# A mixture-of-experts stage: gate and upper layer in three rounded terms with the tokens stationary

## The reference

```python
def hier_moe(x, w_rg, b_rg, w_re, b_re, w1, w3, w2):   # w1, w3: 32 x 1024 x 512, w2: 32 x 512 x 1024
    ...                                                # each token goes to 2 of 32 experts
    def block(args):
        tids, e, w = args
        xb = x_pad[tids]
        hdn = jax.nn.silu(xb @ w1[e]) * (xb @ w3[e])
        return (hdn @ w2[e]) * w[:, None].astype(xb.dtype)
```

## Time and profile before

| | us |
|---|---|
| median of 3 runs | 5024.19 |
| lowest and highest | 5019.49, 5027.0 |
| the profiled execution, its time | 5025.35 |
| its span, first to last instruction | 5024.0 |

### The profile page before, as it was taken

One profiled execution on the slowest core, in us unless ns is written; L12 is line 12 of the kernel. 1 busy time (PEld: TensorE's weight loads), 2 busy tenths in 40 slices (PEclk: granted clock), 3 DMA queues, 4 the chain that ended last, 5 costly groups with the idle time before them and its releaser, 6 DMA issues. The chain is left out here.

```text
span 5024.0 us, 53141 instructions
## 1 busy us (share of the span) xinstructions
PE 4263.0 (85%) x22050; PEld 3515.6 (70%) x22051; DVE 2141.6 (43%) x3609; ACT 1321.3 (26%) x2379; POOL 199.9 (4%) x149
## 2 busy tenths in 40 slices
PE   7877998998887998999777788888499986888884
PEld 5676677777675677777546688888476666888883
DVE  4653334333654234333444455454422243554544
ACT  3202223233202223232432222222222221222222
POOL 0000000000000000000000111111000001111110
PEclk9755579999755569999788899999795577999997
DMA  3100002222100002222003587777320015777783
GB/s 114 51 34 1 1 17 84 84 84 68 52 34 0 1 3 81 84 86 87 24 17 111 204 283 274 276 271 267 109 92 26 22 53 199 275 274 278 277 280 115
DMA packets 278356, 589.38 MB, mean 117 GB/s; under 512 B 31296, under 2 KB 41024, under 8 KB 276960
## 3 DMA queue, kind: packets, MB, share of 16 engines
q1 hardware_dynamic: 259168, 569.08, 32.6%
q0 software_dynamic: 18944, 16.84, 1.1%
HBM read 596.32 MB, written 39.99 MB: 127 GB/s over the span
## 5 line engine op out<-in xcount | busy, mean ns | idle before, releaser
L179 PE MATMUL ps<-r,r 128*128 128x512 f32 x7680 | 1829.7, 398 | 221.6 <-DVE r L2470 101.7
L179 PEld LDWEIGHTS ps<-r,r 128*128 128x128 f32 x7680 | 1445.2, 193 | 592.8 <-issue 169.7
L179 PE MATMUL ps<-mem 128*128 128x128 f32 (+3 forms) x10632 | 1449.0, 300 | 26.2 <-DVE mem L2276 13.5
L179 PEld LDWEIGHTS ps<-mem 128*128 128x128 f32 (+1 forms) x10632 | 1436.9, 219 | 46.5 <-issue 18.4
L703 DVE TENSOR_TENSOR r<-mem,r 128x512 fp32r<-128x512 f32 (+1 forms) x512 | 340.1, 674 | 759.8 <-ACT r L685 759.1
L685 ACT ACTIVATE r<-mem 128x512 fp32r<-128x512 f32 (+1 forms) x512 | 311.9, 618 | 893.9 <-PE ps L179 893.9
L2443 DVE TENSOR_TENSOR r<-mem,r 128x1024 fp32r<-128x1024 f32 x256 | 308.5, 1224 | 220.4 <-ACT r L2405 211.4
L1318 PE MATMUL ps<-mem 64*128 64x512 f32 (+4 forms) x512 | 386.3, 858 | 4.5 <-DVE mem L1477 1.6
L1370 DVE CUSTOM_DVE_ANT_0 mem<-ps,mem 128x512 f32<-128x512 f32 (+3 forms) x224 | 122.7, 549 | 492.1 <-PE ps L1318 459.2
L2405 ACT ACTIVATE r<-mem 128x1024 fp32r<-128x1024 f32 x256 | 263.2, 1053 | 159.9 <-PE ps L179 159.9
L1325 PEld LDWEIGHTS ps<-mem 128*128 128x128 f32 x784 | 129.5, 201 | 247.1 <-issue 226.9
(11 more groups left out here) (282 smaller groups left out, 2553.9 us busy)
## 6 DMA issues: line engine op xcount, KB each, us to landing
mem<-in_w_up SPq DMA_DIRECT2D x80, 2048.0 KB, 8.5
mem<-in_w_down SPq DMA_DIRECT2D x80, 2048.0 KB, 8.1
mem<-in_w_gate SPq DMA_DIRECT2D x64, 2048.0 KB, 8.5
mem<-in_w_in SPq DMA_DIRECT2D x12, 2048.0 KB, 7.9
mem<-in_odd_w_qkv SPq DMA_DIRECT2D x6, 2048.0 KB, 8.2
mem<-in_w_o SPq DMA_DIRECT2D x4, 2048.0 KB, 8.1
mem<-yd SPq DMA_DIRECT2D x8, 1024.0 KB, 8.1
mem<-in_rel SPq DMA_DIRECT2D x32, 224.0 KB, 3.5
```

The source lines that it names most:

```text
L179: r = e.matmul(out, a, b, start=start and i == 0, stop=stop and i == n - 1, skip_group_check=skip)
```

## The change

In `Experts`:

- The weights of an expert are loaded in contiguous rows: partition p gets rows 8p to 8p+7 (for the lower layer 4p to 4p+3), 16 KB in one run, where the gate and upper weights came in runs of 2 KB and the lower in runs of 4 KB. The transposes read every eighth (or fourth) column of their operand to match.
- Gate and upper layer are computed in three rounded terms like the lower one. The turned tokens are split into `XH` (ACT) and `XL` (DVE), both from PSUM, and are stationary; the weights move. All twelve pieces of an expert's weights are split: `high` by ACT into a ring of four buffers (`RING`), `low` by DVE in place, over the loaded weights.
- The hidden layer now comes out with tokens on the partitions, so PE turns it by four transposes (`pe_turn_hidden`), and ACT and DVE split the turned one.
- Silu is one function of ACT; Exp, addition, reciprocal and product go. DVE keeps the product with the upper layer. ACT alone copies results out.
- The lower layer runs one expert later: on PE the order is gate and upper layer of e, transposes of e + 1, lower layer of e - 1, transposes of the hidden layer of e.
- A weight buffer is freed by the last matmul that reads it, for the lower layer too.

```diff
 def expert_chunks(A, out, l):
+    def whole(src):
+        n = src.shape[0] // 128
+        return lambda buf: [(buf, src.rearrange("(p k) n -> p (k n)", k=n))]
...
-            K.frees(("moe", l, e, 0), "ex_gu", l, e, 0)
-            K.frees(("moe", l, e, 1), "ex_gu", l, e, 1)
-            K.frees(("moe", l, e, 2), "ex_wl", l, e, 3)
+            for what in range(3):
+                K.frees(("moe", l, e, what), "ex_mm", l, e, 4 * what + 3)
+        self.turns = []
+        for c in range(NE + 1):
+            if c < NE:
+                self.turns += [(c, c, i) for i in range(8)]
+            if c:
+                self.turns += [(c, c - 1, i) for i in range(8, 12)]
+        self.place = {(e, i): n for n, (_, e, i) in enumerate(self.turns)}
...
+            if e:
+                self.scatter(pool, e - 1)
+        self.scatter(pool, NE - 1)
...
+    def piece(self, e, i):
+
+        K, name = self.K, ("moe", self.l, e, i // 4)
+        o = K.where[name] + 1024 * (i % 4)
+        return K.m(o, 1024), self.WH[self.place[e, i] % self.RING], K.r(o, 1024)
...
-                r = pe.e.transpose(self.turned(half)[:, k, :], self.XG[e % 2][:, c:c + 128], self.K.ident)
+                r = pe.e.transpose(self.turned(half)[:, k, :], self.XG[e % 2][:, 4 * half + k::8], self.K.ident)
...
+    def pe_up(self, pe, e):
+        K, S, l = self.K, self.S, self.l
+        for i in range(8):
+            if i == 0 and e:
+                pe.wait_ge("ex_sg", l, e - 1)
+            if i == 4 and e:
+                pe.wait_ge("ex_h", l, e - 1)
+            if i < 4:
+                pe.wait_ge("ex_xl", l, e, i // 2)
+            pe.wait_ge("ex_wl", l, e, i)
+            _, wh, wl = self.piece(e, i)
+            for j in range(2):
+                k, c = 2 * (i % 4) + j, slice(512 * j, 512 * j + 512)
+                xh, xl = self.XH[e % 2][:, k, :], self.XL[e % 2][:, k, :]
+                r = mm(pe.e, K.bank[i // 4][:, :], ((xh, wh[:, c]), (xl, wh[:, c]), (xh, wl[:, c])), k == 0, k == 7)
+            r.then_inc(*S["ex_mm"](l, e, i))
...
+            r = pe.e.transpose(self.K.bank[4][:, 128 * k:128 * k + 128], self.SG[e % 2][:, k::4], self.K.ident)
+        r.then_inc(*S["ex_ht"](l, e))
...
+    def act_high(self, act, n):
+        _, e, i = self.turns[n]
+        if n >= self.RING:
+            act.wait_ge("ex_mm", self.l, *self.turns[n - self.RING][1:])
+        self.K.wait_weights(act, ("moe", self.l, e, i // 4))
+        w, wh, _ = self.piece(e, i)
+        act.e.activation(wh, w, ACT.Copy).then_inc(*self.S["ex_wh"](self.l, e, i))
...
+        act.e.activation(self.SG[e % 2], self.K.bank[0][:, :], ACT.Silu).then_inc(*self.S["ex_sg"](self.l, e))
...
+        self.act_turned(act, 0)
+        for n, (c, _, i) in enumerate(self.turns):
+            if c == NE and i == 8:
+                self.act_hidden(act, NE - 1)
+                self.act_result(act, NE - 2)
+            self.act_high(act, n)
+            if i == 0 and c:
+                self.act_turned(act, c)
+            elif i == 4 and c:
+                self.act_hidden(act, c - 1)
+                if c >= 2:
+                    self.act_result(act, c - 2)
+            elif c < NE and i == (8 if c else 7):
+                self.act_silu(act, c)
+        self.act_result(act, NE - 1)
...
+            self.dve_low(dve, n)
+            if i == 0 and c:
+                self.dve_turned(dve, c)
+            elif i == 4 and c:
+                self.dve_hidden(dve, c - 1)
+            elif c < NE and i == (11 if c else 7):
+                self.dve_gated(dve, c)
```

More of the change, by code:

```diff
@@ new lines, in pe_down @@
+    def pe_down(self, pe, e):
+        K, S, l = self.K, self.S, self.l
+        if e:
+            pe.wait_ge("ex_y", l, e - 1, 1)
+        pe.wait_ge("ex_hl", l, e)
+        for i in range(8, 12):
+            pe.wait_ge("ex_wl", l, e, i)
+            _, wh, wl = self.piece(e, i)
+            k = i - 8
+            hh, hl = (a[:, 128 * k:128 * k + 128] for a in (self.HH, self.HL))
+            for n in range(2):
+                m = slice(512 * n, 512 * n + 512)
+                r = mm(pe.e, K.bank[6 + n][:, :], ((hh, wh[:, m]), (hl, wh[:, m]), (hh, wl[:, m])), k == 0, k == 3)
+            r.then_inc(*S["ex_mm"](l, e, i))
@@ L2367, in pe, with pe_turn_hidden @@
+    def pe_turn_hidden(self, pe, e):
+        S, l = self.S, self.l
+        pe.wait_ge("ex_h", l, e)
+        if e:
+            pe.wait_ge("ex_hl", l, e - 1)
+        for k in range(4):
+            r = pe.e.transpose(self.K.bank[4][:, 128 * k:128 * k + 128], self.SG[e % 2][:, k::4], self.K.ident)
+        r.then_inc(*S["ex_ht"](l, e))
     def pe(self, pe):
-        K, S, l = self.K, self.S, self.l
         pe.wait_end(self.prev)
         self.pe_turn(pe, 0)
[L2371 to L2383, removed]
+        for e in range(NE + 1):
+            if e < NE:
+                self.pe_up(pe, e)
@@ L2399, in act_high @@
[L2399 to L2413 removed]
+                self.pe_down(pe, e - 1)
@@ new lines, in pe, with act_turned @@
+            if e < NE:
+                self.pe_turn_hidden(pe, e)
+    def act_high(self, act, n):
[5 more added lines that the diff above has]
+        act.e.activation(wh, w, ACT.Copy).then_inc(*self.S["ex_wh"](self.l, e, i))
+    def act_turned(self, act, e):
+        for half in range(2):
+            act.wait_ge("ex_turn", self.l, e, half)
+            act.e.activation(self.XH[e % 2][:, 4 * half:4 * half + 4, :], self.turned(half),
+                             ACT.Copy).then_inc(*self.S["ex_xh"](self.l, e, half))
@@ new lines, in act, with dve_low, dve_turned @@
+        self.act_result(act, NE - 1)
+    def dve_low(self, dve, n):
+        _, e, i = self.turns[n]
+        dve.wait_ge("ex_wh", self.l, e, i)
+        w, wh, wl = self.piece(e, i)
+        dve.e.tensor_tensor(wl, w, wh.bitcast(F32), SUB).then_inc(*self.S["ex_wl"](self.l, e, i))
+    def dve_turned(self, dve, e):
+        for half in range(2):
+            k = slice(4 * half, 4 * half + 4)
+            dve.wait_ge("ex_xh", self.l, e, half)
+            dve.e.tensor_tensor(self.XL[e % 2][:, k, :], self.turned(half), self.XH[e % 2][:, k, :].bitcast(F32),
+                                SUB).then_inc(*self.S["ex_xl"](self.l, e, half))
@@ new lines, in dve @@
+            r = dve.e.memset(self.XG[i], 0.0)
+        r.then_inc(*self.S["ex_zero"](self.l))
+        self.dve_turned(dve, 0)
+        for n, (c, _, i) in enumerate(self.turns):
+            if c == NE and i == 8:
+                self.dve_hidden(dve, NE - 1)
+            self.dve_low(dve, n)
[5 more added lines that the diff above has]
+                self.dve_gated(dve, c)
```

142 lines of the change are left out of this document (41 added, 101 removed).

## The result

| kernel | executions | median us | lowest and highest |
|---|---|---|---|
| before | 4 | 5024.96 | 5019.49, 5027.0 |
| changed | 4 | 4568.3 | 4522.54, 4669.34 |

The ratio of the changed kernel to the kernel before is 0.9004 (95% interval 0.8982 to 0.9025), taken from the two shorter executions of the changed kernel. The profiled one took 4524.55 us, 500.8 less than that of before. Forecast were 347 us less and a range of 4658 to 4785 us, so the measured time lies outside it. One thing has to be known to read any number here: TensorE's clock in the attention of the last layer (stage `odd`) comes out anew in each execution of either kernel, at 0.50, at 1.00 or at the one and then the other, and moves the time by up to 150 us.

The account below looks back on a forecast made before the run. TensorE plus two waits for VectorE bound the 23.8 us expert step. TensorE's 18.23 us plus 0.07 for hand-offs gave 18.3; two stages saved 346.6 us from 5025.35, so 4677 us, range 4658 to 4785.

Parts of the forecast that it names:

- PE's work, 18.23 us: Expert step on TensorE: 72 matmuls 16.67 us, eight transposes 1.04, four hidden transposes 0.52.
- VectorE, 17.4 us: Expert step on DVE: twelve low terms at 1.224 us, 14.69, plus token and hidden low terms and gating product, 2.73.
- DMA: Weight loads of an expert step: 6.57 MB at 400 GB/s, 16.4 us; gate weights land after 13.4 us, in time.
- Bound C: Expert stages: DMA at 349 GB/s sets the step at 18.8 us, 31 us more, 4708 in all; chance 0.07.
- Following one step: Engines traced through one expert step: PE just streams, tightest at the sixth low piece with 0.5 us; step 18.3 us.
- The ends of a stage: Each expert stage, first and last steps included: 593.8 us after against 767.1 before, 173.3 less; two stages 346.6 less.
- Nothing else in the program changes that lies on the path.: Program outside the expert stages: no other change on the path, so only the two stages' 346.6 us are saved.
- rival E: Expert stages: PE falls to half clock, step near 31 us, 450 us slower than before; chance 0.02.
- The range: Whole kernel: from a step of 18.0 us (4658) to B and a little of A or C on top (4785).
- Rival A: Expert stages: VectorE's hand-offs round the ring make the step 19.0 us, 43 us more, 4720 in all; chance 0.20.
- Rival B: Transposes in expert stages: strided stationary loads take twice as long, adding 1.37 us a step, step 19.7, 4764; chance 0.15.
- Rival D: Expert weight loads: three transfers do not overlap in fixed parts, step 25.1 us, 5105 in all, slower than before; chance 0.02.

Follow-up runs that it names:

- The two kernels that make DVE the bound: Changed kernel without low tokens x high weights in gate and upper layer, step 16.74 us; changed kernel with Silu from Exp, addition, reciprocal, product, step 21.42 us.
- the old rows: Changed kernel with the weight loads (2 KB and 4 KB runs) and unstrided transposes of the kernel before: step 18.42 us.
- same-step kernel: Changed kernel with an expert's lower layer in its own step, not one expert later: step 21.73 us in the first stage, 20.96 in the second.

## Why the prediction was wrong

Point by point, by its own steps:

- **PE's work, 18.23 us.** Right: 17.99 us with PE never idle. The 72 matmuls cost 0.2325 us each in one stream of 62 ((14.58 - 0.40) / 61, from 3349.82 us on, 0.40 being the length of the last) and 0.234 over a whole step (72 in 16.88 us between 3329 and 3347 us), against the 0.2315 priced; the twelve transposes cost 0.10 us each in the stream, and I had priced them with the tail of the last one, 0.13.
- **VectorE, 17.4 us.** Too high: 45.6 of 50 us are 16.4 a step. I multiplied the mean duration, 1.224 us, but in a row the next starts before the last has ended: five take 5.84 us, 1.17 each. ACT likewise, three in 2.97 us: 14.7 us, not 16.2. The two kernels that make DVE the bound confirm it, 16.7 and 21.4 us where the sums said 17.4 and 21.9.
- **DMA.** Right: 16.4 us of queue time were forecast, 0.91 of 18.0 are 16.4. Gate weights 13.4 forecast, 13.2 measured. Bound C's mechanism is real but smaller, 18.4 us with the old rows, where I had 18.8. The gathers were not priced at all: they land after 12.7 us and not 5.1, but PE waits for none of them.
- **Following one step.** Right, down to the stop of VectorE before the sixth piece, and confirmed by the kernel with three buffers. The 0.07 us for hand-offs and 0.24 of the sum were not needed.
- **Silu.** 0.58 us, priced 0.6, one table load of 1.28 us a stage.
- **The ends of a stage.** Priced 593.8 us from the end of the first transposes to the last result; the profile has 3377.3 - 2784.4 = 592.9. The first step took 15.4 us (12.7 priced) and the last lower layer 12.4 (10.9), and the 31 steps from the end of one hidden transpose to the last 562.1 (567.3), so misses of either sign cancel in part. The first stage is 174.2 us less and the second 172.1, together 346.3 where 346.6 were forecast.
- **"Nothing else in the program changes that lies on the path."** This is the step that failed. It is true of the instructions and false of the time. It put the difference in the last attention at nothing, and that stretch is 139 us shorter in the profile after, with the same instructions at a clock of 1.00 for 0.50. I had its row in hand, PE busy without a gap at a clock of 0.50, used it for rival E, a fall in the expert stage, and never asked what 0.50 in that stage was worth and whether it was settled. Three executions within 7.5 us made it look so. With the clock there alike in both kernels the forecast saving of 347 us holds: 4873.5 against 4525.9 us is 347.6 at 1.00, and 5023.7 against 4674.9, the medians of executions that lost it, is 349. What decides the clock in an execution stays open.
- **The range.** It took in the bounds of all unknown costs of the change, and nothing for the state of a stage that the change doesn't touch. 150 us belonged on its lower side.
- **Rival A** (VectorE sets the step) didn't happen, with 1.6 us of room instead of 0.8. **Rival B**: the strided loads are slower, 192 ns in a row of eight and 204 for the hidden layer's against 141, so what the Trainium skill ("Advanced Engine Details and Errata", SBUF Cachelines) says of new 16-byte lines agrees with the trace; but a load runs beside the matmul before it, the matmuls still take 1.05 us for eight, and it costs nothing. I had priced a load as if it lay on the path, and my sign for B, a mean load above 0.2 us, was met by the hidden layer's without B being so. **Rival D** (transfers not overlapping): up lands at 18.1 us, not 25.1. **Rival E** (half clock) didn't happen either; its step of 31 us rests on no row, and the counts in the attention, 293 against 157, would make 18.0 us about 34 (an estimate).

## What to carry to other kernels

When PE is the bound with two others just below, let each product's inputs be made one unit of work ahead, count the buffers of the ring by following one step, and price rows of equal instructions by their spacing in a row, not by their mean duration. Before a difference is put down to a change, cut both spans into the same stretches by the first and last start of a few lines: a stretch whose instructions did not change and whose time did is not the change. A short stop of PE at the entry of a stage can cost the stage its clock, and here nine matmuls without use in the stops, for about 5 us, kept it in 6 of 6 executions; at the first `nsa` stage five did not.

## What the runs showed of the hardware

- The same instructions with the same stops (1.47, 0.77 and 0.69 us) kept PE at 1.00 in one execution and dropped it to 0.50 in another, and the attention behind ran at either for hundreds of microseconds with PE busy throughout: 293 or 157 matmuls in 50 us. It came back by itself 41 us after the fall in one profile, and not at all within the stage, some 300 us, in four others.
- In the same-step kernel with a stop of 2.17 us once in 21 to 22 us the mean clock was 0.94 in the first stage and 0.99 in the second, while the kernel before with stops of 1.56 and 1.05 us in 23.8 stayed at 1.00.
- Indirect DMAs of POOL beside 16 KB rows land later: gathers after 12.7 us and scatters after 10.6, where they took 5.1 and 5.8 beside runs of 2 and 4 KB. With the old rows in the changed kernel they took 7.7 and 7.4 us at a DMA share of 0.95, against 0.91. In the kernel before with long rows for gate and up alone, at a share of 0.76, they took 4.9 and 5.7 us. So in these runs long rows delayed them only with the queues nearly full.
- Loading a stationary operand at every eighth fp32 takes 188 to 192 ns instead of 141, at every fourth 204, and hides behind the matmul before it in both kernels.
